# Modulation parts behind projection units on ScalarE's queue, and a recurrence that computes its scores twice

## What is computed

```python
def modulation(cond, w, b):                       # adaLN: 9 vectors of 1024 per layer and token group
    return (silu(cond) @ w + b).reshape(1, 1, 9, 1024)

def modulate_in(x, g_pre, mod, j):  return rmsnorm(x, g_pre) * (1 + mod[3*j + 1]) + mod[3*j]
def gated_residual(x, out, g_post, mod, j, wt):  return x + wt * mod[3*j + 2] * rmsnorm(out, g_post)

def mlstm_scan(q, k, v, log_i, log_f, C0, n0, m0):    # per head (4) and chunk of 128 tokens
    def step(C, n, m):
        s   = (q_b @ k_b.T) * Wd                      # the scores; Wd: decay mask of this direction
        num = w_inter * (q_b @ C) + s @ v_b
        den = w_inter * (q_b @ n) + sum(s)
        h   = num / max(abs(den), exp(-m))
        C_new = w_last * C + (w_k * k_b).T @ v_b      # n_new alike
# h = scan(forward) + flip(scan(flipped inputs)), then rmsnorm per head, times sigmoid(o)
# outputs: y_prompt, y_sample, new_cache_k, new_cache_v, new_state_C, new_state_n, new_state_m
```

## Time and profile before

| what | value |
|---|---|
| time, median of 3 runs (lowest to highest) | 2472.9 us (2469.79 to 2474.32) |
| time of the profiled execution | 2478.73 us |
| its span in the profile | 2476.8 us |
| mean granted TensorE clock, of 2.4 GHz | 0.993 |
| TensorE busy (matmul) | 2416.2 us, 98% |
| VectorE, ScalarE, GpSimd busy | 1747.8, 983.4, 411.8 us |
| bytes moved | 297.95 MB, mean 120 GB/s |

### The profile page before, as it was taken

The page is one execution under the profiler, slowest core; times in us unless marked ns, Lnnn a source line. Parts: engine busy times, 40 slices in busy tenths (PEclk is TensorE's granted clock), DMA queues, the critical chain, the costliest instruction groups (busy, mean ns, idle before and its releaser), DMA issues. The chain is left out here.

```text
span 2476.8 us, 39028 instructions
## 1 busy us (share of the span) xinstructions
PE 2416.2 (98%) x15205; PEld 2210.2 (89%) x15205; DVE 1747.8 (71%) x2449; ACT 983.4 (40%) x1924; POOL 411.8 (17%) x410
## 2 busy tenths in 40 slices
PE   6999999999998999999999999999999999999998
PEld 6997998889887789979988997999899979989997
DVE  5978785666555668778855988686567459866864
ACT  4442443532444454424435442343421154423432
POOL 1120220201214122102203220121200022201211
PEclk9999999999999999999999999999999999999999
DMA  8426334174124534263343426333244323243333
GB/s 260 129 61 219 100 87 139 54 232 111 46 58 164 186 112 131 80 207 86 86 162 112 124 72 209 98 86 115 90 145 137 103 85 103 69 149 99 86 110 112
DMA packets 346646, 297.95 MB, mean 120 GB/s; under 512 B 38219, under 2 KB 296251, under 8 KB 346464
## 3 DMA queue, kind: packets, MB, share of 16 engines
q1 hardware_dynamic: 346464, 295.46, 39.3%
HBM read 280.57 MB, written 14.80 MB: 119 GB/s over the span
## 5 line engine op out<-in xcount | busy, mean ns | idle before, releaser
L2023 DVE TENSOR_TENSOR w_lo<-w_raw,w_hi 128x512 fp32r<-128x512 f32 (+1 forms) x249 | 218.9, 882 | 254.7 <-ACT w_hi L1455 253.3
L1455 ACT ACTIVATE w_hi<-w_raw 128x512 fp32r<-128x512 f32 (+1 forms) x249 | 188.1, 760 | 473.7 <-DMA w_raw<-in_ffn_w_dram 205.5
L949 PE MATMUL psum<-w_hi,act_hi 128*128 128x512 f32 x800 | 319.0, 399 | 2.3 <-DVE w_lo L2023 2.1
L951 PE MATMUL psum<-w_hi,act_lo 128*128 128x512 f32 x800 | 317.1, 396 | 0.0
L950 PE MATMUL psum<-w_lo,act_hi 128*128 128x512 f32 x800 | 317.0, 396 | 0.0
L1082 PE MATMUL psum<-hT_hi,w_hi 128*128 128x320 f32 x912 | 281.9, 309 | 0.5 <-DVE z_quarters L2309 0.5
L1083 PE MATMUL psum<-hT_lo,w_hi 128*128 128x320 f32 x912 | 281.8, 309 | 0.0
L1084 PE MATMUL psum<-hT_hi,w_lo 128*128 128x320 f32 x912 | 281.8, 309 | 0.0
L949 PEld LDWEIGHTS psum<-w_hi,act_hi 128*128 128x128 f32 x800 | 150.6, 188 | 44.0 <-DVE w_lo L2023 5.5
L1082 PE MATMUL psum<-t_hi,w_hi_more 128*128 128x320 f32 x608 | 187.9, 309 | 0.0
L1084 PE MATMUL psum<-t_hi,w_lo_more 128*128 128x320 f32 x608 | 187.9, 309 | 0.0
(11 more groups left out here) (303 smaller groups left out, 5906.0 us busy)
## 6 DMA issues: line engine op xcount, KB each, us to landing
w_raw<-in_ffn_w_dram SPq DMA_DIRECT2D x96, 512.0 KB, 4.5
w_raw_next<-in_ffn_w_dram SPq DMA_DIRECT2D x80, 512.0 KB, 5.4
w_raw<-in_ffn_w_dram SPq DMA_DIRECT2D x148, 256.0 KB, 3.0
ada_tile_ffn<-in_ada_w_dram SPq DMA_DIRECT2D x56, 512.0 KB, 4.5
ada_direct<-in_ada_w_dram SPq DMA_DIRECT2D x40, 512.0 KB, 6.0
w_raw<-in_ab_w_in_dram SPq DMA_DIRECT2D x28, 512.0 KB, 4.3
w_raw<-in_sc_w_in_dram SPq DMA_DIRECT2D x24, 512.0 KB, 4.0
x_kept_rows<-x SPq DMA_DIRECT2D x20, 512.0 KB, 5.7
```

The source lines that it names most:

```text
L949: mm(out, a_hi, b_hi, start=first, stop=False)
L951: return mm(out, a_lo, b_hi, start=False, stop=final)
L1455: A(dst, src, ACT.Copy).then_inc(w_hi_ok, 1)
L2023: V.tensor_tensor(d_, a, b.bitcast(F32), ALU.subtract).then_inc(w_lo_ok, 1)
```

## The change

1. The two direct parts of sublayer 1 leave the recurrence. Two steps each come behind projection units 3, 4, 5, 6, 8, 9, 10 and 11.
2. All direct tiles are loaded, and all direct rows stored, by ScalarE's queue in place of SyncE's. In sublayer 1 the loads come behind ScalarE's own evacuation of units 2 (four), 4, 5, 6, 7, 9 and 10 (two each), the rows behind those of units 7 and 11. In the FFN sublayers steps 0 to 3 are loaded behind the first SiLU, steps 4 to 7 behind the third, and the rows are stored behind a later split. A load waits in ScalarE's list for the buffer it fills.
3. `x` is loaded again at projection unit 15, in place of the output projection.
4. The recurrence keeps no scores. `SCORE_STEPS` has steps 5, 6 and 7 too; ScalarE's three copies go, and VectorE reads all scores from PSUM.
5. VectorE's splits of the output projection's units 1 to 3 go from between the recurrence's steps to behind its last one; ScalarE's third goes ahead of its last `head_squares`.
6. SyncE: the weight loads of units 1 to 5 in a row, then the stores of the states, the wait, `gate`, the columns of the next sublayer, and all other weights. The output projection's first unit takes its five tiles in the order 4, 0, 1, 2, 3.

Core of the diff:

```diff
-REC_AT = {2: (0, 2), 3: (2, 5), 4: (5, 8), 5: (8, 10), 6: (10, 12), 7: (12, 14), 8: (14, 16)}
-REC_LOADS = {3: (4, 8), 4: (8, 10), 5: (10, 16)}
+AB_AT = {u: range(2 * i, 2 * i + 2) for i, u in enumerate((3, 4, 5, 6, 8, 9, 10, 11))}
+AB_ROWS = {7: 0, 11: 1}
+AB_LOADS = {2: range(4), 4: range(4, 6), 5: range(6, 8), 6: range(8, 10), 7: range(10, 12), 9: range(12, 14), 10: range(14, 16)}
...
-SCORE_STEPS = [0, 1, 2, 3, 8]
-SCORE_KEPT = {5: 2, 6: 1, 7: 0}
+SCORE_STEPS = [0, 1, 2, 3, 5, 6, 7, 8]
...
 # SyncE, sublayer 1
-                        load_out(s, ab_w_out[0], 0, ph, 1, 3)
-                        for k in range(4):
-                            load_direct(s, 0, k)
-                        for u in range(3, AB_SPLIT):
-                            load_out(s, ab_w_out[0], 0, ph, u, u + 1)
-                            for j in range(*REC_LOADS[u]):
-                                load_direct(s, j // KD, j % KD)
+                        load_out(s, ab_w_out[0], 0, ph, 1, AB_SPLIT)
...
                         load_gate(s)
-                        load_out(s, ab_w_out[0], 0, ph, AB_SPLIT, AB_SPLIT + 2)
-                        for z in range(2):
-                            store_direct(s, z)
-                        for t in range(NT):
-                            reload_x(s, t)
-                        sp.wait_ge(mod_stored, STORED(DB[s] + 1))
                         load_cols(s + 1)
-                        load_out(s, ab_w_out[0], 0, ph, AB_SPLIT + 2)
+                        load_out(s, ab_w_out[0], 0, ph, AB_SPLIT)
...
 # TensorE, projection and recurrence
                     modulation(ph, u)
+                    for j in AB_AT.get(u, ()):
+                        direct_step(1, j // KD, j % KD)
...
                     if q + 2 in SCORE_STEPS:
                         products(q + 2)
-                    if q == 2:
-                        pe.wait_ge(ml_st, 3)
-                        pe.wait_ge(sc_kept, 3)
-                    for j in range(*REC_AT.get(q, (0,))):
-                        direct_step(1, j // KD, j % KD)
...
 # ScalarE: FFN sublayers
                     A(halves(sg[:]), IN_V[nb % 2], ACT.Silu).then_inc(in_evac[nb % 2], 1)
+                    for k in (range(4) if i == 0 else range(4, KD) if i == 2 else ()) if s in DIRECT else ():
+                        load_direct(s, 0, k)
...
 # ScalarE: sublayer 1
                     evac_unit(u)
+                    for j in AB_LOADS.get(u, ()):
+                        load_direct(1, j // KD, j % KD)
+                    if u in AB_ROWS:
+                        direct_out(1, AB_ROWS[u])
+                        store_direct(1, AB_ROWS[u])
...
 # VectorE, behind the recurrence
-                    if q in (1, 3, 5):
-                        split(ph["nout"] + (q + 1) // 2, shape="out", u=(q + 1) // 2)
                 for n in range(2, NT):
+                    split(ph["nout"] + n - 1, shape="out", u=n - 1)
                     head_scale(n)
```

More of the change, by code:

```diff
@@ L14 @@
-import itertools
 from contextlib import ExitStack, contextmanager
@@ L360, in build @@
         SUM_BANK = {"ffn": (1, 1), "ab": (4, 6), "sc": (6, 6)}
-        DIRECT_AREA = lambda s, z: (0, z * MW) if s == 1 else (7, 0)
+        DIRECT_BANK = {0: 7, 1: 5, 2: 7, 3: 7}
         OUT = [[4, 5, 6, 7, 0], [1, 2, 3, 4, 5]]
@@ L533, in direct_done @@
         def direct_done(eng, s, z, k):
[L535 to L538, removed]
+            eng.wait_ge(direct_used, KD * parts.index((s, z)) + k + 1)
+        DROWS = lambda s, z: 2 + 4 * (parts.index((s, z)) + 1)
+        DSTORED = lambda s: 64 * sum(len(DIRECT[q]) for q in DIRECT if q <= s)
         def whole_h(eng, s):
@@ L664, in store_mod_rows @@
                     dma(dst, rows[32 * i:32 * i + 2, :]).then_inc(mod_stored, 16)
[L666 to L682, removed]
             def keep_x(s, t):
@@ L733, in load_pairs @@
                         keep_x(s, t)
-                    for k in DIRECT_LOADS.get(2 * i + 1, ()) if s in DIRECT else ():
-                        load_direct(s, 0, k)
                 for g in range(ph["g0"], ph["g1"]):
@@ L747, in load_pairs @@
                         late_rows(plan[s][0])
[L748 to L752, removed]
+                    if s == 0 and g == ph["g0"] + 1 and not ph["half"]:
+                        load_slow()
             def load_out(s, w, row0, ph, u0=0, u1=99):
@@ L856, in _ @@
                             load_mods(ph, u)
+                            if u == 15:
+                                direct_done(sp, s, 1, KD - 1)
+                                for t in range(NT):
+                                    reload_x(s, t)
                             if u == 17:
@@ L1087, in direct_step @@
             def direct_step(s, z, k):
-                pe.wait_ge(direct_loaded[k % 4], 16 * (2 * parts.index((s, z)) + k // 4 + 1))
-                bank, c0 = DIRECT_AREA(s, z)
-                out = lambda i: PS[32 * i:32 * i + 2, bank, c0:c0 + MW]
+                di = parts.index((s, z))
+                pe.wait_ge(direct_loaded[k % 4], 16 * (2 * di + k // 4 + 1 + (0 if k % 4 else di + 1)))
+                out = lambda i: PS[32 * i:32 * i + 2, DIRECT_BANK[s], 0:MW]
                 cols = lambda i: slice(i * MW, (i + 1) * MW)
                 if k == 0:
-                    pe.wait_ge(bias_in, BIAS(DB[s] + z))
+                    if z:
+                        pe.wait_ge(kept_by_act, DROWS(s, z - 1))
                     for i in range(4):
@@ L1098, in direct_step @@
                     last = mm(out(i), csil[:, :, k], direct[s][k % 4][:, cols(i)], start=False, stop=(k == KD - 1))
-                last.then_inc(mod_mm if k == KD - 1 else direct_used, 1)
+                last.then_inc(direct_used, 1)
             def modulation(ph, u):
@@ L1174, in out_phase @@
                         turns({3: (0, 1), 4: (2,), 5: (3,)}[k])
-                    for t in ((0, 1, NT - 1, 2, 3) if ph.get("ab") and k == 0 else range(NT)):
+                    for t in ((NT - 1, 0, 1, 2, 3) if ph.get("ab") and k == 0 else range(NT)):
                         if k == 0:
@@ L1657, in mixed_in @@
                     t_split(s, ph, 3)
+                if ph["plain"] and s in DIRECT:
+                    store_direct(s, 0)
                 for g in range(g0, g1):
@@ L1748, in keep_turned @@
                         act.wait_ge(na_o[p], n)
+                    else:
+                        act.wait_ge(direct_stored, DSTORED(1))
                     cols = slice(0 if head_tile(p, n)[1] < CT else NLOC, NS)
@@ L1856, in mixing @@
                     if n == NT - 1:
-                        direct_out(1, 0)
-                        direct_out(1, 1)
+                        split(ph["nout"] + 3, shape="out", u=3)
                     head_squares(n)
```

100 lines of the change are left out of this document (50 added, 50 removed).

## The result

The changed kernel took 2481.05 us (median of 6 runs, 2478.48 to 2482.53), the kernel before 2472.68 (6 runs). The ratio is 1.0036 with an interval of 1.0026 to 1.0046: **slower by 8.4 us**, where 8 us faster were forecast and the range ended at 2474.

The account below looks back on a forecast made before the run. TensorE, busy in 98% of the span, was taken as the bound. Terms -20.3 + 2.5 + 3.4 + 6.3 + 0 = -8.1 us against the profiled 2478.7 gave 2470.6, or 2464.8 us on the median's scale; range 2454 to 2474.

Parts of the forecast that it names:

- part 1: Recurrence, 56.8 us before: splits, tiles and direct matmuls go, three score sets come; -20.3 us, between -24 and -16.
- Recurrence after: Length of the changed recurrence: 36.5 us, with TensorE setting the pace in steps 3 to 5 at 3.85 us each.
- Projection: Sublayer 1's projection takes in 8.9 us of direct work, partly hidden in idle time: +2.5 and +3.4 us.
- The first pair: Ahead of the gates' unit: 1.56 us of direct work hidden in TensorE's wait of 2.44; late tile costs +2.5 us.
- The wait at unit 12: Projection: of TensorE's 3.75 us wait for VectorE's sums, 1.9 us credited, plus 2.0 for the slow clock behind it.
- Output projection: Behind the recurrence: TensorE idles 4.8 us ahead of unit 6, then 1.5 of slower clock; +6.3 us, between 0 and 9.
- SyncE's wait: Behind the recurrence: SyncE waits 8.1 us for the stored states, holding back the weights of units 6 and 7.
- FFN tiles: FFN sublayers: tiles of steps 4 to 7 asked for 5 to 6 us ahead; 0, at most 2 us per part.
- rival 2: Whole kernel: recurrence keeps 3 us more, tiles cost 7.6, SyncE's wait 7; all given back, about 0, 2473 us; chance 0.16.
- rival 3: Projection starves for DMA: 15 us of waits, 3 at lower clock, 8.9 of work; +13, 2486 us; chance 0.09.

Follow-up runs that it names:

- base_again: The kernel before, unchanged, run again for a second profile; ratio 1.0001 to the kernel before.
- early_states: The changed kernel with SyncE storing the final states right behind the load of unit 3's weights, units 4 and 5 loaded behind them; ratio 1.0047.
- splits_inside: The changed kernel with the weight splits of the output projection's units 1 to 3 back between the recurrence's steps; 2478.34 us, ratio 1.0006.

## Why the prediction was wrong

- **The starting point: the step that failed most.** The forecast was 8.1 us faster; the profiles of the change and of base_again differ by 7.9 the other way. Of these 16.0 us, 5.4 lie in the recurrence, 4.8 in the projection, 1.1 in the output projection, and 4.7 in the start and the rest, which were put at 0. The 5.4 come from the term of part 1 that credits the change with all of 56.8 us: it took the wait of 4.60 us for `scoresT` and the slow clock behind it as if each execution of before had them. -20.3 was forecast; the runs show -21.1 against the first profile and -14.9 against the second. Of seven profiles with such a split in the recurrence, only the first has it at 7.35 us; in the others that split took 0.84 to 1.64. I had read that the profiled execution was 5.8 us above the median, and took it for an even stretch of 0.24%. It was mostly one place, and the very one that the change works on.
- **Recurrence after: right.** 36.5 forecast, 35.75 measured twice within 0.05. Steps 3 to 6 started 3.57 to 3.65 us apart, not 3.85, and TensorE had no idle time between them: it set the pace, as forecast.
- **Projection: mechanism right, size wrong.** +5.9 forecast, +10.7 measured. The first pair was not hidden: the gap that should hold it ended 4.9 us later (counted from the start of sublayer 0's last output phase), not 2.5, and TensorE ran at half clock behind it, which I had not counted (1.1 us more for the gates' unit, 1.6 in the second profile). The wait at unit 12 did give back its 3.75 us, more than the 1.9 I took, but a slow stretch stood there still, at 600 to 604, and a wait for the attention's `probs` that before does not have came behind it (0.81 us at 632, 1.29 in the second profile).
- **Output projection: right for the wrong chain in part.** +6.3 forecast, +7.4 measured, with 5.07 us of idle time for 4.8, and 7.15 in the second profile. I charged SyncE's wait, and its steps came close: the load of unit 6 was forecast at 22.2 us and stood at 22.9. (3.0 + 3.0 + 1.3 in that sum is 7.3, not 7.4.) But early_states shows that weights asked for behind the stores come late without that wait too, and splits_inside that it was the moved splits that put the stores 9.8 us later.
- **FFN tiles.** 0 forecast with a bound of 2 us per part. TensorE waited 0.50 and 0.84 us for tiles in sublayer 0 and 0.63 twice in sublayer 3, 2.6 us in all, within that bound. The start lost 1.3 us and the rest 3.4 against base_again, but both lie within what profiles of unchanged FFN code differ by, so no more than these waits can be put down to the change.
- **Rivals.** The outcome lies between rivals 2 and 3. None of the waits was as long as rival 3 asked. The rule that the prediction takes from the Trainium skill ("DMA: Bandwidth & Descriptors", section "Issuing engines are not separate DMA queues") agrees with this trace: with both issuers at work, four us moved 410 GB/s at a share of 1.01, where one issuer had moved 407 GB/s at 1.03 in 500 to 504 of the kernel before, and the tiles of the other queue came late. A comparison of the two queues in sublayer 1, with all else equal, was not tried.

## What to carry to other kernels

Take two profiles of the kernel before, above all when the profiled time is off the median, compare each one's own time with the median, and forecast from waits that both show; a wait that one execution has can't be counted in full. When an operation moves, look at what was released by it: here the splits between the recurrence's steps freed the buffers for the next weights, and moving them behind it held back the stores of the states and all that SyncE asks for behind these. A queue's order is worth checking before its work is moved: in the timed runs, one row of a load table (0.9985) was not told apart from the whole restructuring with its three losses mended (0.9979).

## What the runs showed that I had not expected

- One VectorE operation with two SBUF operands took 1.64 or 7.35 us at the same place in two executions of one program, and a score from SBUF 6.53 us where 0.68 to 1.76 is usual, each under GpSimd's run of operations without a gap. The Trainium skill ("SBUF — State Buffer", section "Who interferes with whom") calls the shared port pair an exclusive lock, and says that who issues first decides who waits; here VectorE was held over five or six GpSimd operations of 1.06 to 1.28 us, and the same split went either way in two executions of one program. With no such operation in the recurrence it took 35.75 to 35.8 us in six profiles.
- Weights asked for right behind the stores of the final states (the normalisers leave SBUF as 128x4x1, single float32 numbers) took 14 us to be usable; the changed kernel's list of issues has 3.6 us as the median landing of these weights. That these small pieces are the reason was not tested.
- TensorE's granted clock fell to 0.50 (1.2 GHz) behind the 5.9 us of idle time, but also at 600 to 604 in the changed kernel, behind 2 us of tiny matmuls with no idle time, and behind sublayer 1 in one of two executions of before that had the same waits there.
